# A decoder layer on one Trainium2 core: the experts' gate-up weights in 1 MB transfers, with a reordered start and router

## What is computed

```python
logits = (ht @ w_router) + b_router            # 256 x 32
top_logits, top_idx = lax.top_k(logits, 4)
gates = softmax(top_logits)
...
gu = xb @ w_gate_up[e] + b_gate_up[e]          # 1024 x 2048 for each e
gate = jnp.minimum(gu[..., :D_FF], 7.0)
up = jnp.clip(gu[..., D_FF:], -7.0, 7.0)
act = (up + 1.0) * (gate * jax.nn.sigmoid(gate * 1.702))
return act @ w_down[e] + b_down[e]             # 1024 x 1024
```

## Time and profile before

| what | us |
|---|---|
| median of 3 runs (lowest to highest) | 1254.5 (1254.37 to 1255.22) |
| the profiled execution's own time | 1253.78 |
| its span, from the first to the last instruction | 1251.9 |
| PE busy in the span | 1167.4 (93%) |
| time that the packets of SP's transfers took, as a share of 16 DMA engines' span | 87.6% |

### The profile page before, as it was taken

The page is one execution under the profiler, slowest core; times in us unless marked ns, Lnnn a source line. Parts: engine busy times, 40 slices in busy tenths (PEclk is TensorE's granted clock), DMA queues, the critical chain, the costliest instruction groups (busy, mean ns, idle before and its releaser), DMA issues.

```text
span 1251.9 us, 15336 instructions
## 1 busy us (share of the span) xinstructions
PE 1167.4 (93%) x6156; PEld 614.0 (49%) x6156; DVE 390.7 (31%) x704; ACT 274.1 (22%) x417; POOL 7.5 (1%) x27
## 2 busy tenths in 40 slices
PE   7999999999999999988988999899999998999996
PEld 6998887898634433333333333333433333343432
DVE  5887687546312111111111112102111111122112
ACT  6655566345211101010000011001101011011102
POOL 1000100000000000000000000000000000000000
PEclk9999999999999999999999999989999999999999
DMA  9454333478899999999999999999999999999996
GB/s 317 176 196 141 135 113 137 163 269 344 305 427 430 428 428 428 428 428 429 429 428 428 429 428 430 429 427 427 429 428 429 429 429 428 393 430 429 427 425 263
DMA packets 55654, 454.28 MB, mean 363 GB/s; under 512 B 6396, under 2 KB 6564, under 8 KB 30532
## 3 DMA queue, kind: packets, MB, share of 16 engines
q1 hardware_dynamic: 55440, 453.74, 87.6%
q10 hardware_dynamic: 180, 0.07, 0.0%
HBM read 452.74 MB, written 1.05 MB: 362 GB/s over the span
## 4 chain that ended last, share of the span: by engine, by line
PE 55%; DMA 41%; SPq 1%; DVE 1%; issue 1%; ACT 0%; DVEq 0%; ACTq 0%
DMA ring<-in_moe_w_down 41%; PE ps L886 13%; PE ps L910 11%; PE ps L563 3%; PE ps L565 3%; PE ps L564 3%; PE ps L578 2%; PE ps L920 2%; PE ps L579 2%; PE ps L580 2%; PE ps L862 2%; PE ps L551 1%; PE ps L695 1%; PE ps L897 1%; SPq L434 1%
## 5 line engine op out<-in xcount | busy, mean ns | idle before, releaser
L910 PE MATMUL ps<-ring,wring 128*64 128x512 f32 x960 | 216.5, 597 | 53.7 <-DMA ring<-in_moe_w_down 53.7
L886 PE MATMUL ps<-ring,wring 128*64 128x512 f32 x1024 | 223.3, 594 | 0.0
L1030 ACT ACTIVATE wring<-ps 128x512 f32<-128x512 f32 (+2 forms) x101 | 52.5, 535 | 501.5 <-PE ps L886 430.9
L910 PEld LDWEIGHTS ps<-ring,wring 128*64 128x64 f32 x960 | 65.1, 137 | 193.3 <-issue 111.6
L1747 DVE COPY wring<-ps 128x512 f32<-128x512 f32 x32 | 22.1, 692 | 405.3 <-PE ps L886 405.3
L886 PEld LDWEIGHTS ps<-ring,wring 128*64 128x64 f32 x1024 | 72.1, 137 | 139.7 <-issue 139.6
L1755 DVE TENSOR_TENSOR wring<-ps,bguT 128x512 f32<-128x512 f32 x64 | 41.2, 686 | 301.2 <-PE ps L897 301.2
L886 PE MATMUL ps<-mid,wring 128*64 128x512 f32 x512 | 114.7, 601 | 1.0 <-DVE wring L1755 1.0
L1030 ACT ACTIVATE ysb<-ps 128x512 f32<-128x512 f32 x36 | 21.5, 597 | 265.2 <-PE ps L910 251.0
L886 PEld LDWEIGHTS ps<-mid,wring 128*64 128x64 f32 x512 | 35.9, 138 | 68.7 <-issue 68.7
L862 PEld LDWEIGHTS ps<-wring 128*128 128x128 f32 x480 | 55.8, 191 | 23.5 <-issue 23.5
(11 more groups left out here) (313 smaller groups left out, 1402.7 us busy)
## 6 DMA issues: line engine op xcount, KB each, us to landing
ring<-in_moe_w_gate_up SPq DMA_DIRECT2D x64, 2048.0 KB, 23.1
ring<-in_moe_w_down SPq DMA_DIRECT2D x60, 2048.0 KB, 25.5
mid<-in_moe_w_gate_up SPq DMA_DIRECT2D x32, 2048.0 KB, 23.5
wring<-in_moe_w_gate_up SPq DMA_DIRECT2D x16, 2048.0 KB, 26.4
hs<-in_moe_w_gate_up SPq DMA_DIRECT2D x16, 2048.0 KB, 27.9
wring<-in_ssd_w_in SPq DMA_DIRECT2D x10, 2048.0 KB, 8.0
wring<-in_xa_w_kv SPq DMA_DIRECT2D x4, 2048.0 KB, 8.0
wring<-in_ssd_w_out SPq DMA_DIRECT2D x4, 2048.0 KB, 7.8
```

Source lines behind the costliest of these rows:

```text
L886: last = mm(ps[a][SLOTS * half:SLOTS * (half + 1), :], xs[:, m, c % 2, :], w[:, kk, c0:c0 + 512], start=s + kk == 0, stop=s + kk == GP)
L910: last = mm(ps[D_BANK][SLOTS * half:SLOTS * (half + 1), :], act[:, k, :], w[:, kk, 512 * half:512 * (half + 1)], start=k == 0, stop=k == K ...
L1030: return nc.scalar.activation(out_, in_, func, **kw)
```

## The change

- **Gate-up rows.** Each gate-up piece is loaded by two transfers of 1 MB, one for each of the two rows of a partition (`load_gate_up_row`), with a semaphore for each; PE waits for a row and counts `gu_used` after each row.
- **Start.** Two loads of `x` have a semaphore each; piece 0 is loaded in halves, and `first_projection` (in place of `project_T`) takes all outputs' first half before their second. The parameters' transposes move behind the first eight of the norm, DVE's constants behind the norm, and PE first runs 17 matmuls on constants.
- **Early slots.** `xo`, `prT` and `lgT` are laid out so that halves of slots come free earlier; `wo_half` tells SP. The load into `hs` no longer waits for `hot_ok`. The first row of expert 2 is loaded in halves.
- **Router.** The residual goes into PSUM by four ScalarE copies (`sum_in`) instead of PE's matmuls; the mask comes from replacing the four maxima and comparing (`match_replace`, `not_equal`) instead of indices; `onehot` follows `rank` at once; PE runs matmuls on constants while it waits (`keep_warm`); a quarter of the first gather is moved into the first expert.
- **After the loop.** Expert 27's first two gate-up pieces now stand ahead of expert 25's down weights.

```diff
-        g_ready = [sem(f"g_ready{s}") for s in range(2 * GP)]
+        g_ready = [[sem(f"g_ready{s}_{kk}") for kk in range(2)] for s in range(2 * GP)]
...
+        def load_gate_up_row(sp, e, odd, s, kk):
+            n = GP * odd + s
+            sp.dma_start(gu_w(n)[:, kk:kk + 1, :], gu_dram[e, s, :, kk:kk + 1, :]).then_inc(g_ready[n][kk], 16)
+
         def load_gate_up(sp, e, odd, s):
-            n = GP * odd + s
-            sp.dma_start(gu_w(n), gu_dram[e, s, :, :, :]).then_inc(g_ready[n], 16)
+            load_gate_up_row(sp, e, odd, s, 0)
+            load_gate_up_row(sp, e, odd, s, 1)
...
+        def load_down_rows(sp, e, s, half):
+            rows = slice(2 * half, 2 * half + 2)
+            sp.dma_start(dn_w(s)[:, rows, :], dn_dram[e, s, :, rows, :]).then_inc(d_ready[s], 16)
...
-                sp.dma_start(h[:, t, :], x[P * t:P * (t + 1), :]).then_inc(ld_x, 16)
+                sp.dma_start(h[:, t, :], x[P * t:P * (t + 1), :]).then_inc(ld_x[t], 16)
...
-            sp.dma_start(wpiece(0), pieces[0]).then_inc(w_ready[0], 16)
+            sp.dma_start(wpiece(0)[:, 0:4, :], pieces[0][:, 0:4, :]).then_inc(w_first, 16)
+            sp.dma_start(wpiece(0)[:, 4:8, :], pieces[0][:, 4:8, :]).then_inc(w_ready[0], 16)
...
             sp.dma_start(g_ffn, ffn_norm.partition_broadcast(P)).then_inc(ld_g, 16)
             sp.wait_ge(pv_ps, XH)
             load_gate_up(sp, 1, 1, 0)
+            sp.wait_ge(wo_half, 1)
+            load_down_rows(sp, 0, 0, 0)
             sp.wait_ge(wo_ps, 8)
-            load_down(sp, 0, 0)
+            load_down_rows(sp, 0, 0, 1)
+            sp.wait_ge(wo_half, 2)
+            load_gate_up_row(sp, 1, 1, 1, 0)
+            load_gate_up_row(sp, 1, 1, 2, 0)
             sp.wait_ge(wo_ps, 10)
-            load_gate_up(sp, 1, 1, 1)
-            load_gate_up(sp, 1, 1, 2)
-            sp.wait_ge(hot_ok, 1)
+            load_gate_up_row(sp, 1, 1, 1, 1)
+            load_gate_up_row(sp, 1, 1, 2, 1)
+            sp.wait_ge(normed, 2 * 3 + TC)
+            sp.wait_ge(lg_ps, 1)
+            load_gate_up_row(sp, 1, 1, 3, 1)
             sp.wait_ge(sums_ok, 1)
-            load_gate_up(sp, 1, 1, 3)
+            load_gate_up_row(sp, 1, 1, 3, 0)
+            for a in range(2):
+                sp.wait_ge(*((gu_used if a else gu_part), 1))
+                sp.dma_start(gu_w(0)[:, 0:1, 1024 * a:1024 * (a + 1)],
+                             gu_dram[2, 0, :, 0:1, 1024 * a:1024 * (a + 1)]).then_inc(g_ready[0][0], 16)
+            for r in range(1, GR):
+                sp.wait_ge(gu_used, r + 1)
+                load_gate_up_row(sp, 2, 0, r // 2, r % 2)
             sp.dma_start(bdn[0:NE, :], b_down).then_inc(ld_bdn, 16)
...
+            def reload_gate_up(e, i, c, pieces_=range(GP)):
+
+                for s in pieces_:
+                    for kk in range(2):
+                        sp.wait_ge(gu_used, 2 * GR * i + (GR * (c - 2) + 2 * s + kk + 1))
+                        load_gate_up_row(sp, e, c % 2, s, kk)
...
-            reload_gate_up(2, 0, 2)
             with sp.Fori(0, PAIRS - 4, 1) as i:
                 for c in (1, 2):
                     reload_gate_up(2 * i + (c + 2), i, c + 2)
                     reload_down(2 * i + c, i, c)
-            for e in range(NE - 7, NE - 2):
+            reload_gate_up(NE - 5, 0, NE - 5, (0, 1))
+            reload_down(NE - 7, 0, NE - 7)
+            reload_gate_up(NE - 5, 0, NE - 5, (2, 3))
+            for e in range(NE - 6, NE - 2):
                 reload_down(e, 0, e)
                 reload_gate_up(e + 2, 0, e + 2)
             sp.wait_ge(cnt_ps, 1)
             sp.dma_start(g_fin, final_norm.partition_broadcast(P)).then_inc(ld_gf, 16)
             for n in range(2 * DP):
-                sp.wait_ge(gu_used, GP * (NE - 2) + n + 1)
                 for half in range(2):
+                    sp.wait_ge(gu_used, GR * (NE - 2) + 2 * n + half + 1)
                     rows = slice(2 * half, 2 * half + 2)
                     sp.dma_start(dn_last(n)[:, rows, :],
-                                 dn_dram[NE - 2 + n // DP, n % DP, :, rows, :]).then_inc(dl_ready[2 * n + half], 16)
+                                 dn_dram[NE - 2 + n // DP, n % DP, :, rows, :]).then_inc(g_ready[n][half], 16)
...
+            pe.wait_ge(cst_step, 1)
+            for _ in range(WARM):
+                mm(ps[0][:, 0:P], ones, ones, start=True, stop=True)
+            pe.wait_ge(cst_step, 2)
+
+            def parameters(t):
+                pe.wait_ge(ld_rows, 112)
+                tr(ps[7][:, 0:120], rows_a[0:120, :], ident[0:120, 0:120])
+                tr(ps[7][:, 128:176], rows_b[0:48, :], ident[0:48, 0:48]).then_inc(par_ps, 1)
...
-            norm_transposes(0, xn0, 2)
+            norm_transposes(0, xn0, 2, parameters)
...
+            def first_projection():
+
+                w = wpiece(0)
+                pe.wait_ge(par_sb, 1)
+                for half in range(2):
+                    pe.wait_ge(*((w_ready[0], 16) if half else (w_first, 16)))
+                    for b in range(2):
+                        for m in range(2):
+                            for k in range(4 * half, 4 * half + 4):
+                                if b == m == 0:
+                                    pe.wait_ge((nt_dve, nt_act)[k // 2 % 2], 2 * half + k % 2 + 1)
+                                c0 = (2 * b + m) * P
+                                last = mm(u_out(0, b, m), w[:, k, c0:c0 + P], xT[:, k, :],
+                                          start=k == 0, stop=k == KD - 1)
+                        if half:
+                            last.then_inc(u_ps, 1)
...
-                split_tokens(W_O + 1, t, 6 + t, xo).then_inc(wo_ps, 1)
+                if half == 0:
+                    last.then_inc(wo_half, 1)
+            for half in range(2):
+                for t in range(TC):
+                    last = split_tokens(W_O + 1, t, 5 + 2 * t, xo[half], k0=-4 * half, ks=range(4 * half, 4 * half + 4))
+                    if half:
+                        last.then_inc(wo_ps, 1)
+                if half == 0:
+                    last.then_inc(wo_half, 1)
...
+            def keep_warm(bank, times):
+
+                for _ in range(times):
+                    mm(ps[bank][:, 0:2 * P], ones, cst[:, 2:4, :], start=True, stop=True)
+
+            pe.wait_ge(hT_dve, 1)
+            keep_warm(1, 2)
...
+            keep_warm(1, 1)
...
-            for t in range(TC):
-                for n in range(2):
-                    last = mm(ps[4 + 2 * t + n][:, :], ident, h[:, t, 512 * n:512 * (n + 1)], start=True, stop=True)
-            last.then_inc(sums_ok, 1)
+            keep_warm(1, 3)
...
+            keep_warm(0, 2)
+            pe.wait_ge(sums_ok, 1)
...
-            def gate_up(i, c):
+            def gate_up(i, c, first=False):
...
-                    pe.wait_ge(g_ready[n], 16 * i + 16 * (c // 2 + 1))
                     w = gu_w(n)
                     for kk in range(2):
+                        pe.wait_ge(g_ready[n][kk], 16 * i + 16 * g_loads(n, kk, c))
                         m = 4 * (s // 2) + 2 * kk + s % 2
                         for a in range(2):
                             for half in range(2):
                                 c0 = 1024 * a + 512 * half
                                 last = mm(ps[a][SLOTS * half:SLOTS * (half + 1), :], xs[:, m, c % 2, :],
                                           w[:, kk, c0:c0 + 512], start=s + kk == 0, stop=s + kk == GP)
-                    last.then_inc(gu_used, 1)
+                            if first and s + kk + a == 0:
+                                last.then_inc(gu_part, 1)
+                        last.then_inc(gu_used, 1)
+                        if first and s == 1 and kk == 0:
+                            first_gather(1, (2, 3))
...
             fn(nrm[:, 5, 1:2], nrm[:, 5, 0:1], ACT.Identity, bias=eps[:, 0:1], scale=1.0 / D)
+            sum_in(0, 1)
...
-            hT_out(1)
+            sum_in(1, 1).then_inc(sums_ok, 1)
...
             add_part(0, 0)
             add_part(0, 1)
             add_part(1, 0)
-            norm_chunk(3, 0, xn, h, g_ffn)
             add_part(1, 1)
             hT_out(0)
             hT_out(1)
-            norm_chunk(3, 1, xn, h, g_ffn)
+            norm_chunk(3, 0, xn, h, g_ffn)
+            dve.wait_ge(std, 2 * 3 + TC)
+            v.reciprocal(rst[:, 3, 1:2], nrm[:, 3, 1:2])
+            dve.drain()
...
             v.tensor_scalar(gsum[:, :, 0], mx8[:, :, 0], -1.0, None, ALU.mult).then_inc(lmax, 1)
+            v.memset(mx8[:, :, TOPK:8], 3e38)
+            dve.drain()
             for t in range(TC):
-                v.max_index(ix8[:, t, :], mx8[:, t, :], lg[:, t, :])
-            dve.drain()
-            v.tensor_copy(ix4f[:, :, :].rearrange("p n t -> p t n"), ix8[:, :, 0:TOPK])
-            dve.drain()
-            v.tensor_tensor(eq.rearrange("p (m e) -> p m e", e=NE),
-                            iota0[:, :].unsqueeze(1).to_broadcast([P, TOPK * TC, NE]),
```

(25 more changed lines are left out.)

187 lines of the change are left out of this document (90 added, 97 removed).

## The result

The changed kernel takes 1256.55 us (median of 19 runs, 1255.63 to 1259.99) against 1254.50 (19 runs, 1253.67 to 1255.57): a ratio of 1.0017, with a 95% interval of 1.0011 to 1.0024. It is slower by 2.05 us, where 6.3 were forecast.

The account below looks back on a forecast made before the run. The prediction took full DMA engines, 428 GB/s, as the bound. 13 - 0.7 - 1.5 - 2.2 - 2.3 = +6.3 us on the profiled 1253.78 gave 1260.1, or 1260.8 as median; range 1256 to 1264, for 8 in 10 1253 to 1265.

Parts of the forecast that it names:

- What bounds it: Whole kernel: DMA engines are full at 428 GB/s in the steady state, 29.4 us an expert, where PE needs 26.1.
- no slice under 415 from 330 on: Sign in the GB/s slices: from 330 us on, none of them would read below 415 GB/s.
- rival B: Same mechanism but small: packet cost at its lower bound, 8 us, or larger start gains; 1253 to 1257 us; chance 0.12.
- 8 KB runs: Gate-up and `hs` loads, 254 MB: 8 KB in one run instead of 16 KB costs 13 us, bounds 8 and 16.
- gap behind the loop: Stretch 1062 to 1072: two gate-up pieces ahead of the `w_down` wait remove the gap, gaining 2.3 us.
- Start: Kernel start: earlier statistics and transposes, less the parameters' two transposes, move everything up to `hs` 0.7 us earlier.
- Router: Router: a shorter mask computation lets the `hs` load be issued 1.5 us earlier, bounds 0.5 and 3.
- Gap at the first expert: Stretch 334 to 346: earlier `gate_up` and earlier freed slots leave no gap behind the `hs` load, gaining 2.2 us.
- Tail: Last eight loads: already 8 KB runs, only queued earlier and waiting in a full queue anyway; effect 0.
- A: Run length costs nothing, 419 GB/s being a trait of the last 20 us; only gains stand, 1247.8 us; chance 0.13.
- C: Steady state: if loads in flight are limited by number, gaps arise in each expert; 1289 us at one us each; chance 0.03.
- the estimate of 3.4 us: Packet overhead from the Trainium skill: 3.5 ns each, 968 more packets on each engine; set aside for the trace's 14 ns.

## Why the direction was right and the size was not

**What bounds it** held: the DMA share is 0.99 to 1.02 in every window from 334 on, and the lead in bytes at 1230 us is the difference of the spans. The mean distance in the chain, the twice as many issues of 1024 KB and the missing dip at 1065 came as written, and so did "no slice under 415 from 330 on", but for the slice at 409. (Of the slices before, "at 427 to 430, with one slice at 393", the last but one reads 425.) The 1256.55 us lie in the range of 1256 to 1264, at its very edge, and as well in rival B's; of the 6.3 us forecast a third came.

By its own terms, forecast against measured, for the profiled executions:

| term | forecast | measured | from |
|---|---|---|---|
| 8 KB runs | +13 | +9.1 | the split alone: 9.3 - 0.2 behind |
| lead at the first expert (start, router, gap) | -4.4 | -5.3 | bytes at 345 us |
| gap behind the loop | -2.3 | -2.9 | bytes from 1050 to 1085, less 0.4 of run length |
| dip at 354 to 362 (0.6 of it the later `b_down` load) | none | +1.0 | 8 x (1 - 370/424); the split alone has 418 there |
| dip behind the loop, near 1098 (the new order's) | none | +0.7 | bytes from 1085 to 1230, less 1.4 of run length |
| sum | +6.3 | +2.6 | span: +2.7 |

**The step that failed** is "254 MB at 419 instead of 428 GB/s are 606 - 593 = 13 us", mis-sized by 3.9 us, where the whole sum is off by 3.7; the other errors cancel. The mechanism was right. The 419 came from a stretch of 17 us in which 8 KB loads ran alone. The prediction had a second reading of nearly the same stretch, 422 GB/s, worked out that it gives 9 (254 MB at 422 against 428 are 8.4, against 429 9.8), and set it aside for rounding. The steady state of 424 is two parts gate-up and one part down: with the down weights at 428, 3/424 = 2/r + 1/428 gives r = 422. The 2 us by which the first stretch is longer move about 396 GB/s ((17 x 419 - 15 x 422) / 2), and they alone pull 422 down to 419. That doesn't settle all: the changed kernel shows 419 in its own 1221 to 1236, so short stretches there read up to 3 low; why is open. The prediction said 422 for the steady state as its sign and got 424, which is the same error. Two terms that it put at nothing without a price stand in the table too: the `b_down` load behind the reloads of expert 2, and a dip that the new order makes itself (the prediction has only "The gap goes").

**Start, 0.7 forecast.** The projection started 2.8 us earlier. "The 17 matmuls on constants fall into idle time" was true and missed what they do: by the experiment without them they take 1.5 us from the transposes. The rest, 1.2 to 1.3, goes with the earlier statistics: ACT starts them at 4.78 in its timeline and not at 6.04; no run takes this apart from the other changes at the start. Of the 1.5 us of the matmuls 0.7 reaches the `hs` load. Still the attention ends 2.7 us earlier, and 2.0 without the matmuls, where the projection had started only 1.2 earlier: 0.8 us more came between the two, from a part of the change that no run isolates.

**Router, 1.5 forecast.** The `hs` load was issued 4.5 us earlier, 2.7 of them from the earlier end of the attention, so the router gave about 1.75. `gate_up` started 4.5 us earlier and not 1.7, since it inherits all of this. `keep_warm` (eight matmuls, not seven as in the prediction) kept the granted clock at 1.00, which stood in no term of the prediction; without it 2.5 us are lost.

**Gap at the first expert, 2.2 forecast.** "335.6, while the `hs` load runs until about 337.4: no gap" failed. With all else earlier, the queue had run down before the `hs` load already (share 0.66 from 328 to 331), the quarter pieces came at 333.0, and the window 334 to 346 still moves 369 GB/s: 12 x (1 - 369/428) = 1.7 us missing, 0.5 us less than before and not 2.2. So two gains that were added up, an earlier `hs` load and no gap behind it, share the same us in part; the sum of the three came out 0.9 better only because the start gave more.

**Gap behind the loop, 2.3 forecast**: alone the new order gave 2.0 net. In the changed kernel it gave 2.9, and 0.7 came back near 1098, so 2.2 net.

**Tail, 0**: the load that the last chain waits for lands 2.7 us later than before and the span is 2.7 longer. It held.

**Rivals.** A (run length costs nothing, 1247.8) fell: the steady state is at 424, and with 16 KB runs put back the kernel lands at 1248.99, near the time that A gave. The rule of the Trainium skill named with it (DMA: Bandwidth & Descriptors, Rules for kernel authors) is met by all these transfers, and 1% of the rate still hangs on the run length. B (same mechanism, small, 1253 to 1257) tells best what happened, by both ways it named: the run length near its lower bound and a larger gain at the start. Its upper end, 9 - 6.7 = +2.3 us, is nearly the measured +2.6, though not term by term: larger gains and the two unforeseen dips cancel. C fell: no dip that comes back with each expert, and no slice from the thirteenth to the 39th under 416. The fixed cost for a packet that the Trainium skill has (DMA: Bandwidth & Descriptors, Why small descriptors are slow), from which the estimate of 3.4 us came, falls short of the 9.1 measured.

## What to carry to other kernels

In a stretch where the DMA engines are full, splitting a transfer so that a semaphore comes earlier is paid for with every byte if it shortens the contiguous run of a partition; split only the few transfers whose early release fills a gap, and keep the long runs elsewhere. Price such a cost with a long stretch and the mix of traffic that it will have, and when two readings of one stretch differ, carry both into the sum. Add gains along one chain as a lead in bytes at one moment, not one by one. In a list that is issued in order, look at what stands behind a wait: loads whose slots are free already belong ahead of it.

## What was not expected of the hardware

- Transfers that write 64 of the 128 partitions: 241 GB/s with full engines in a mix that is two thirds such transfers, where those of 128 partitions alone reach 428; the kernel took 2020 us.
- 128x128 transposes: 0.23 us each where PE had done little before, 0.13 behind 5.6 us of matmuls. The rows show a granted clock of 1.00 for both, so they do not say whether it is the clock. In the router, where the gather's 24 matmuls took 5.13 against 2.92 us, they show 0.50 to 0.62 against 1.00.
- A load of 128 KB over 32 rows, issued into a full queue at 347.5 us, cost some 0.6 us beyond the 0.3 us of its bytes (0.131 MB / 428 GB/s), in the dip at 354 to 362 us.
